# One 512-column matmul for the high weights, and a reduction that adds the two halves

## The reference

```python
hn = _rmsnorm(h, norm1_g[layer])
proj = hn @ w_in[layer]
...
h = h + jnp.concatenate([attn_out, ssm_out], axis=-1) @ w_out[layer]
h = h + (jax.nn.silu(hn @ w_gate[layer]) * (hn @ w_up[layer])) @ w_down[layer]
...
proj = h @ w_in
merged = (gates[:, :, 0] * (y_lru @ w_br_lru) + gates[:, :, 1] * (y_attn @ w_br_attn)
          + gates[:, :, 2] * (y_mem @ w_br_mem))
x = x + rmsnorm(merged @ w_out, norm_mix_post)
u = jnp.square(jax.nn.relu(hm @ w_up))
x = x + rmsnorm(u @ w_down, norm_mlp_post)
```

## Time and profile before

| | |
|---|---|
| median of 3 runs | 3399.64 us (3398.23 to 3400.7) |
| span of the profiled execution | 3399.2 us |
| PE busy, weight loads busy | 96%, 94% of the span |
| DVE busy, ACT busy, POOL busy | 63%, 45%, 16% |
| chain that ended last | PE 87%, DVE 9%, issue 2%, ACT 2% |
| DMA | mean 171 GB/s, at most 212 in one of 40 slices |

### The profile page before, as it was taken

How to read it: one execution, slowest core, us unless ns; L and a number is a source line. 1 busy time by engine, 2 the same in 40 slices (tenths; PEclk the granted TensorE clock), 3 DMA queues, 4 the chain that set the end, 5 groups by cost and what they waited for, 6 DMA issues and landing times.

```text
span 3399.2 us, 67239 instructions
## 1 busy us (share of the span) xinstructions
PE 3279.3 (96%) x26280; PEld 3212.2 (94%) x26280; DVE 2136.7 (63%) x2409; ACT 1530.1 (45%) x1885; POOL 532.6 (16%) x511
## 2 busy tenths in 40 slices
PE   5999999999999999899999999999997999999997
PEld 5898889999999999899999999999997999999997
DVE  7788887755555555857865666455556655555555
ACT  3444445454334344337753556444333333333342
POOL 5343443300000000703430000000014000000002
PEclk9999999999999999999999999999998999999999
DMA  6444444655555555555555444555553455555553
GB/s 212 151 154 147 156 142 143 193 184 167 194 184 180 176 182 171 162 193 173 167 195 179 154 149 161 178 174 174 181 173 118 161 186 178 187 180 186 180 185 124
DMA packets 169036, 580.49 MB, mean 171 GB/s; under 512 B 19072, under 2 KB 20864, under 8 KB 168896
## 3 DMA queue, kind: packets, MB, share of 16 engines
q1 hardware_dynamic: 160272, 558.16, 49.8%
q0 software_dynamic: 3408, 10.75, 0.9%
q10 hardware_dynamic: 5216, 9.64, 0.8%
HBM read 571.13 MB, written 7.34 MB: 170 GB/s over the span
## 4 chain that ended last, share of the span: by engine, by line
PE 87%; DVE 9%; issue 2%; ACT 2%; DMA 0%; ACTq 0%; DVEq 0%; POOL 0%; POOLq 0%; SPq 0%
PE gemm_psum L326 26%; PE gemm_psum L327 26%; PE gemm_psum L328 26%; DVE weights_lo L1104 3%; PE gemm_psum L320 1%; PE gemm_psum L321 1%; PE gemm_psum L322 1%; PE bank_b L338 1%; ACT weights_hi L688 1%; DVE projections L1375 0%; DVE x_lo L1127 0%; PE bank_s L570 0%; PE bank_b L591 0%; PE bank_s L602 0%; DVE late L1217 0%
## 5 line engine op out<-in xcount | busy, mean ns | idle before, releaser
L1104 DVE TENSOR_TENSOR weights_lo<-weights,weights_hi 128x1024 fp32r<-128x1024 f32 (+2 forms) x1104 | 1349.9, 1236 | 968.6 <-ACT weights_hi L688 962.6
L688 ACT ACTIVATE weights_hi<-weights 128x1024 fp32r<-128x1024 f32 (+2 forms) x1104 | 1109.9, 1018 | 1427.0 <-PE gemm_psum L328 1262.3
L326 PE MATMUL gemm_psum<-x_hi,weights_hi 128*128 128x256 f32 x5120 | 1467.4, 287 | 68.3 <-DVE weights_lo L1104 41.7
L327 PE MATMUL gemm_psum<-x_lo,weights_hi 128*128 128x256 f32 x5120 | 1455.9, 284 | 0.0
L328 PE MATMUL gemm_psum<-x_hi,weights_lo 128*128 128x256 f32 x5120 | 1455.5, 284 | 0.0
L326 PEld LDWEIGHTS gemm_psum<-x_hi,weights_hi 128*128 128x128 f32 x5120 | 985.2, 192 | 81.0 <-issue 37.4
L327 PEld LDWEIGHTS gemm_psum<-x_lo,weights_hi 128*128 128x128 f32 x5120 | 985.3, 192 | 0.8
L328 PEld LDWEIGHTS gemm_psum<-x_hi,weights_lo 128*128 128x128 f32 x5120 | 985.1, 192 | 0.0
L326 PE MATMUL gemm_psum<-u_hi,weights_hi 128*128 128x256 f32 x2880 | 826.0, 287 | 17.6 <-DVE weights_lo L1104 15.2
L327 PE MATMUL gemm_psum<-u_lo,weights_hi 128*128 128x256 f32 x2880 | 816.2, 283 | 0.0
L328 PE MATMUL gemm_psum<-u_hi,weights_lo 128*128 128x256 f32 x2880 | 816.1, 283 | 0.0
(11 more groups left out here) (338 smaller groups left out, 2553.6 us busy)
## 6 DMA issues: line engine op xcount, KB each, us to landing
weights<-in_w_branch SPq DMA_DIRECT2D x192, 512.0 KB, 3.3
weights<-in_w_gu SPq DMA_DIRECT2D x176, 512.0 KB, 3.4
weights<-in_w_up SPq DMA_DIRECT2D x128, 512.0 KB, 3.5
weights<-in_w_down SPq DMA_DIRECT2D x128, 512.0 KB, 3.3
weights<-in_w_dn SPq DMA_DIRECT2D x64, 512.0 KB, 3.3
weights<-in_w_in_qk SPq DMA_DIRECT2D x32, 512.0 KB, 3.3
weights<-in_w_mem_k SPq DMA_DIRECT2D x32, 512.0 KB, 3.5
weights<-in_w_mem_v SPq DMA_DIRECT2D x32, 512.0 KB, 3.4
```

The lines of the kernel that those rows point to most:

```text
L326: pe.matmul(o, wh, xh[:, kk, :], start=first, stop=False)
L327: pe.matmul(o, wh, xl[:, kk, :], start=False, stop=False)
L688: act.activation(HI[:, j % RING, 0:g.kt * GC], RAW[:, j % RING, 0:g.kt * GC], ACT.Copy)\
L1104: dve.tensor_tensor(LO[:, j % RING, cols], RAW[:, j % RING, cols], HI[:, j % RING, cols].bitcast(f32), ALU.subtract).then_inc(lo_done, 1)
```

## The change

`weights_hi` and `weights_lo`, and the high and low activations, become one tensor each with the two parts next to each other (`WS`, `XS`, `US`); the old names are views of them. One matmul of 512 columns then streams both: high weights by (high, low) activations, or, with `tokens_out`, high activations by (high, low) weights. It writes a full PSUM bank: the product with the high parts in columns 0 to 255, the other in 256 to 511. The third product stays a 256-column matmul into the first half. `taken` is now an instruction: a `tensor_reduce` over a view that has the two halves innermost reads 128 x 1024 values of PSUM and writes 128 x 512 into SBUF (`halves[p]`), then DVE waits for it and the callers read `halves[p]`. In `glu` DVE does this too, and ACT waits for it. The full diff:

```diff
--- before.py
+++ after.py
@@ -141,12 +141,12 @@
             return ctx.enter_context(nc.semaphore(name))
 
         RAW = sb("weights", [P, RING, UNITS * GC])
-        HI = sb("weights_hi", [P, RING, UNITS * GC], f32r)
-        LO = sb("weights_lo", [P, RING, UNITS * GC], f32r)
-        XH = sb("x_hi", [P, KT, T], f32r)
-        XL = sb("x_lo", [P, KT, T], f32r)
-        UH = sb("u_hi", [P, KT, T], f32r)
-        UL = sb("u_lo", [P, KT, T], f32r)
+        WS = sb("weights_split", [P, RING, 2, UNITS * GC], f32r)
+        XS = sb("x_split", [P, KT, 2, T], f32r)
+        US = sb("u_split", [P, KT, 2, T], f32r)
+        HI, LO = WS[:, :, 0, :], WS[:, :, 1, :]
+        XH, XL = XS[:, :, 0, :], XS[:, :, 1, :]
+        UH, UL = US[:, :, 0, :], US[:, :, 1, :]
         H = sb("residual", [P, KT, T])
         ZP = sb("projections", [P, 2 * KT, T])
         Q2 = sb("late", [P, 4096])
@@ -163,6 +163,8 @@
         acc = sb("squares", [P, 2, T])
         small = sb("small", [P, 24, 32])
         consts = sb("consts", [P, 4])
+        HS = sb("halves", [P, 2, 2 * T])
+        halves = [HS[:, n, :].rearrange("p (a t) -> p a t", a=2) for n in range(2)]
 
         def vec(name, a=0, n=None):
             start, size = VEC[name]
@@ -248,6 +250,7 @@
         pool_link, dve_link, act_link, sq_step = sem("pool_link"), sem("dve_link"), sem("act_link"), sem("sq_step")
 
         hi_done, lo_done, mm_done = sem("hi_done"), sem("lo_done"), sem("mm_done")
+        summed = sem("summed")
 
         angle_in, theta_done, angle_done, bbar_done = sem("angle_in"), sem("theta_done"), sem("angle_done"), sem("bbar_done")
         bt_done, bt_copied, bt_out, cyc_half = sem("bt_done"), sem("bt_copied"), sem("bt_out"), sem("cyc_half")
@@ -307,25 +310,21 @@
                 wait(pe, lo_done, b(SLOTS, SLOTS * g.first + j + 1))
                 if j % UNITS == 0:
                     wait(pe, evac[p], b(1, g.first))
-                xh, xl, off = operands
+                xs, off = operands
                 for n in range(2):
                     for k in range(g.kt):
                         kk = off + (j % UNITS) * g.kt + k
                         first, end = j % UNITS == 0 and k == 0, j % UNITS == UNITS - 1 and k == g.kt - 1
-                        o = GP[:, 2 * p + n, 0:T]
+                        both, o = GP[:, 2 * p + n, :], GP[:, 2 * p + n, 0:T]
                         if tokens_out:
                             cols = slice(k * GC, (k + 1) * GC)
-                            wh, wl = HI[:, j % RING, cols], LO[:, j % RING, cols]
-                            ah, al = xh[:, kk, n * P:(n + 1) * P], xl[:, kk, n * P:(n + 1) * P]
-                            pe.matmul(o, ah, wh, start=first, stop=False)
-                            pe.matmul(o, al, wh, start=False, stop=False)
-                            mm = pe.matmul(o, ah, wl, start=False, stop=end)
+                            tokens = slice(n * P, (n + 1) * P)
+                            pe.matmul(both, xs[:, kk, 0, tokens], WS[:, j % RING, :, cols], start=first, stop=False)
+                            mm = pe.matmul(o, xs[:, kk, 1, tokens], HI[:, j % RING, cols], start=False, stop=end)
                         else:
                             cols = slice(k * GC + n * P, k * GC + (n + 1) * P)
-                            wh, wl = HI[:, j % RING, cols], LO[:, j % RING, cols]
-                            pe.matmul(o, wh, xh[:, kk, :], start=first, stop=False)
-                            pe.matmul(o, wh, xl[:, kk, :], start=False, stop=False)
-                            mm = pe.matmul(o, wl, xh[:, kk, :], start=False, stop=end)
+                            pe.matmul(both, HI[:, j % RING, cols], xs[:, kk, :, :], start=first, stop=False)
+                            mm = pe.matmul(o, LO[:, j % RING, cols], xs[:, kk, 0, :], start=False, stop=end)
                 mm.then_inc(mm_done, 1)
 
             def ssm_in(q, i):
@@ -421,7 +420,7 @@
                         mm = pe.transpose(bank[:, q % 2, n * P:(n + 1) * P], b_bar[n][:, 4 * q:4 * q + 4, :], ident[:, :])
                 mm.then_inc(bt_done, 1)
 
-            x, u = (XH, XL, 0), (UH, UL, 0)
+            x, u = (XS, 0), (US, 0)
             for b, _ in in_u.stretches(pe, peel=True):
                 for j in range(SLOTS):
                     if b() == 0 and j < 4:
@@ -478,7 +477,7 @@
                 for j in range(SLOTS):
                     if b() == 0 and j in (0, 2, 3):
                         pe.wait_ge(yl_done, (1, 2, 2, 3)[j])
-                    units(glu, b, j, (XH, XL, UT))
+                    units(glu, b, j, (XS, UT))
             for b, _ in out_ssm.stretches(pe, peel=True):
                 for j in range(SLOTS):
                     if isinstance(b(), int) and b() == 0 and j in (0, 2):
@@ -847,9 +846,9 @@
             def glu_events(slot, b):
                 if slot in (3, 7):
                     gidx = 2 * b() + slot // 4
-                    act.wait_ge(mm_done, SLOTS * (glu.first + b()) + slot + 1)
+                    act.wait_ge(summed, 2 * (glu.first + b()) + slot // 4 + 1)
                     for n in range(2):
-                        ins = act.activation(ZP[:, UT + 2 * gidx + n, :], GP[:, 2 * (slot // 4) + n, 0:T], ACT.Sigmoid,
+                        ins = act.activation(ZP[:, UT + 2 * gidx + n, :], halves[slot // 4][:, n, :], ACT.Sigmoid,
                                              bias=vec("b_glu", 2 * gidx + n, 1))
                     ins.then_inc(evac[slot // 4], 1)
                 if slot == 7:
@@ -1106,8 +1105,13 @@
 
             def taken(g, b, slot):
 
+                p = slot // 4
                 wait(dve, mm_done, b(SLOTS, SLOTS * g.first + slot + 1))
-                return GP[:, 2 * (slot // 4):2 * (slot // 4) + 2, 0:T]
+                wait(dve, evac[p], b(1, g.first))
+                dve.tensor_reduce(halves[p], GP[:, 2 * p:2 * p + 2, :].rearrange("p n (h t) -> p n t h", h=2), AX.X, ALU.add)\
+                   .then_inc(summed, 1)
+                wait(dve, summed, b(2, 2 * g.first + p + 1))
+                return halves[p]
 
             def row(v):
 
@@ -1348,6 +1352,8 @@
                 lower_part(3, 7, 8)
 
             def glu_events(slot, b):
+                if slot in (3, 7):
+                    taken(glu, b, slot)
                 if slot == 7:
                     dve.wait_ge(evac[1], glu.first + b() + 1)
                     t, y = slice(UT + 4 * b(), UT + 4 * b() + 4), slice(4 * b(), 4 * b() + 4)
```

## The result

The changed kernel takes 3425.98 us (median of 5 runs, 3410.24 to 3432.15) against 3399.64. The ratio is 1.0067, with a 95% interval of 1.005 to 1.0085. The forecast was 3317 us; the time lies in its range, on the side to which it gave 0.21. The runs of after spread over 0.6%, those of before over 0.07%; that has a cause of its own (e10).

What follows compares the result with a forecast made beforehand. The prediction took PE to bound the kernel, through the spacing of its matmuls. From 3399.6 us it took 130 saved (18 ns on 7200 sets) and added 47 lost, mainly to the reduction: 3317 us, range 3250 to 3430.

Steps and rivals of the forecast that it cites:

- The bound: Whole kernel: the time is PE's, set by matmul spacing of 120 ns; PE busy 96% of the span, DVE 63%.
- The size of the 512-column matmul: Weight matmuls: 222 ns for 512 columns plus 120 for 256, a set from 360 to 342, saving 130 us.
- the 6 paid once: 512-column matmul: some 6 ns over array time belong to the matmul, paid once and not per column, so 216 + 6.
- rival 2: Weight matmuls: excess goes with f32r columns, set stays 360 ns, 3447 us; deciding point a set of 353.5; chance 0.21.
- Where the reduction is bare: Stages where PE's work doesn't cover the added DVE reduction: together 47 us lost.
- in_u, mem_k, mem_v, out_attn: Stages where DVE gets 10.8 us more each: no saving on their sets, 0 to 20 us lost, 10 taken.
- lru_in, lru_gate, in_q2, branch 0: LRU-side projections and first branch: counted as PE-limited, gaining 18 ns a set, no reduction cost.
- the boundaries: Eight stage boundaries: PE waits for the last DVE result of the stage before, 1.35 us more each, 10.8 us.
- residual adds with two SBUF inputs: Adds in out_ssm and the last down projection: slowed beside POOL's work by 0 to 0.6 us each, 5 us taken.
- rival 3: 512-column matmul in between, at 229 to 233 ns: 3370 to 3397 us, near no change; chance 0.11.
- Rival 1: 512-column matmul costs nothing over its array time, 216 ns, set 336 or less: 3274 us; chance 0.29.
- Rival 4: The strided reduction on DVE costs 2.5 us: 46 us more on the forecast, 3363 us; chance 0.04.

Runs made afterwards that it cites:

- e10: Second run of the changed kernel with the change only in stages where PE is the limit, three matmuls and no reduction elsewhere: 3347.38 us, ratio 0.9856.
- e2: The reduction added to the kernel before, with three 256-column matmuls kept and the second writing the upper half of the bank: 3480.22 us, ratio 1.0236.
- e6: e1 with the wide matmul cut from 512 to 384 columns, so half of the product with the lo activations isn't computed: 2968.39 us.
- e4: e1 with the split weights and activations in bfloat16 in place of f32r: 3150.7 us.
- e12: The kernel before with its split weights and activations in bfloat16, three 256-column matmuls a set as before: 3172.96 us.
- e7: The changed kernel with the sum over two engines, ACT copying the upper halves out of PSUM and DVE adding the lower ones: 3419.07 us, ratio 1.0067.
- e1: The changed kernel without the reduction, the second half of each PSUM bank computed but left out of the result: 3326.64 us, ratio 0.9796.

## Why the prediction was wrong, by its steps

**The bound, right.** PE bounds the full stages: in e2, with DVE at 71% of the span instead of 63%, they kept their 360 ns.

**The size of the 512-column matmul, wrong; the first failed step.** "222, the 6 paid once, since the f32 row is nearest in array time and in load." It measured 230.0 or 236.7, the short one 116.7 instead of 120, the set 346.7 or 353.3 instead of 342. The step behind it was that the load's share of the 13 ns hides behind a longer matmul, as in the f32 rows. It does not: in the faster spacing the wide matmul keeps the full 13.3 ns, as e6 shows for 384 and 512 columns, and the slower adds 6.7. The change takes away one such 13.3 of three, or half of one. The f32 row shares array time and load, but draws half as many operand columns in a ns; the prediction said this itself, under rival 2, and still let the row set the value. e4 and e12 show that the excess is one of the f32r type. The row of its own type, the 256-column matmul with 13.3 over its array time, would have given 226.7 + 120 = 346.7, the faster spacing to the digit; the slower stood in no row. On the 5920 sets of full stages without LRU side and branch 0, 18 ns would have been 107 us, less some 11 at boundaries, so -96; after shows -38.6 there (in_qk, in_v, first FFN but its last down stage, k, v, qm, branches 1 and 2, out2, last FFN): 57 us of the miss.

**Where the reduction is bare, wrong; the second.** e2 puts it at 80 us against 47:
- in_u, mem_k, mem_v, out_attn: forecast 10, measured 24.8. The range was 0 to 20, the choice its middle. DVE's slack there (107 of 126 us) could not be used: the side work is a chain over PE, ACT, DVE and POOL, and PE waits for it at the head of its own queue (the waits above). e4 shows besides that these stages are hardly bound by PE's matmuls. e7 bears it out: with 689 ns on DVE in place of 1222 less than half of the loss is left in mem_k, mem_v and out_attn.
- lru_in, lru_gate, in_q2, branch 0: counted among the stages that gain 18 ns a set (23 us), with nothing for the reduction; e2 shows +19.0. The 59% of the earlier trace rows are a mean over the branches, and the three LRU-side stages (1431 to 1739 us, DVE busy for 221 of 307.5) are in none of its stretches. e4, where in_q2 hardly shrank, shows that PE's sets did not bound it. Branch 0 and branch 2 of before apart, by stretch, show the difference:

```profile
1878.90:2103.60 224.70, 224.70 (x1753) 218.37 (x1752) 151.20 (x245) 127.07 (x208) 0.00 (x0) 1.00 0.44 150
```
```profile
2319.80:2508.10 188.30, 184.49 (x1538) 184.28 (x1536) 106.08 (x104) 77.02 (x79) 0.00 (x0) 1.00 0.54 181
```

DVE is busy for 67% and 56%, with 245 and 104 instructions. After the change PE waits in branch 0 for the softmax beside it (before it had no wait there):

```profile
PE bank_s L569 <- DVE work L1566: 6.4, 8, 0.9
PE bank_y L583 <- DVE work L1591: 1.6, 8, 0.2
```

- out_ssm with glu 15.8 (forecast 10.8), the last down stage 10.2 (10.8), the boundaries 11.4 in the six other stages that end late (10.8 in eight): right within 5 us, but partly by luck. The waits grew by less than the 11 us that were to show (3.2 to 10.7, and 8.3 to 16.2 in after), and the matmuls at 1.2 GHz behind them, on which the forecast put nothing, made up for it.
- residual adds with two SBUF inputs, forecast 5: nothing. They measured 691 to 694 ns, hardly more than with one PSUM input (674). POOL's work there waits for the add itself (L1809 behind L1379, 71.1 us in 8 times), so it runs beside the neighbour that follows, not beside the add.

On the stages outside the full ones the forecast had about +14 us and after shows +64.8: 51 us of the miss. With the 57 above this is the whole of 3426 - 3317 = 109 within 1 us. The two errors have the same sign; none hides the other. The time fell into the range because that reached almost to the full rival 2.

**The sum of parts.** -73 (e1) and +80 (e2) would give 3407; after has 3426. In the table the stages that are bare show nearly the same with wide and with narrow matmuls (mem_v +9.6 and +10.3, out_ssm +12.9 both): a faster PE there only waits longer, and what e1 gained in them is lost. Most of the rest lies in how the two spacings fell: the last FFN at 353.3 in after and at 346.7 in e1 is 14 us. Since e1 and after both spread over more than 20 us for that reason, their medians can't be added up more closely.

**Rivals.** Rival 2 forecast the direction, but not by its mechanism: an excess that goes with the columns gives 240 + 120 = 360 for 512 + 256 and 300 for 384 + 256, and 346.7 to 353.3 and 293.3 were measured. Its deciding point, a set of 353.5 ns at a loss of 47, was not reached either; the kernel was slower because the loss was 80. So the 0.21 came true by the cost of the reduction, which no rival had. On PE's part the sets lie between the edge of the forecast's own neighbourhood (338 to 347) and rival 3 (349 to 353). Rival 1 (216) is excluded for f32r, and is exact for bf16. Rival 4 is excluded by the 1222 ns.

By the Trainium skill's rule of N/2.4 + 2.5 ns (TensorE: Matmul & The Clock Gate, section Back-to-back issue gap) 256 and 512 columns would take 109.2 and 215.8 ns, an estimate. The bf16 runs agree to 0.3 ns (109.2 and 216), the f32r runs do not (120 or 116.7, and 230 to 236.7).

**Right:** the reduction at 1.22 us, the last FFN's cover (no wait, chain 4.5 us), the releaser in out_ssm and the last down stage, and no limit from DMA.

## What to carry to other kernels

Price an operation that the trace doesn't show by a row of the same operand type, here the excess over array time of the matmul beside it; array time and load size are not enough, and a neighbour of another type is a bound, not a value. Price work added to a half-idle engine stage by stage, from who waits for whom at the head of the bounding engine's queue: a mean of 59% hid one branch at 67%, where the reduction was bare, and one at 56%, where it was covered. Add to each new wait the matmuls at the lower clock that follow it. And when a change wins in some stages and loses in others, choose by stage: the same two edits gave +0.7% everywhere and -1.3 to -1.4% where they pay.
